# Feed-forward up units: one 512-column product for both operand parts, halves added on VectorE; two norms' squares summed on VectorE

## The reference

```python
def rms_norm(x, g):
    xf = x.astype(jnp.float32)
    y = xf * lax.rsqrt(jnp.mean(xf * xf, axis=-1, keepdims=True) + EPS)
    return (y * g.astype(jnp.float32)).astype(x.dtype)

def swiglu(h, w_in, w_out):          # w_in 1024 x 5632, w_out 2816 x 1024
    a, b = jnp.split(h @ w_in, 2, axis=-1)
    return (jax.nn.silu(a) * b) @ w_out

h = rms_norm(x, norm_mix_g);  x = x + hybrid_mixer(h, ...)
h = rms_norm(x, norm_x_g);    x = x + cross_attention(h, mem, ...)
h = rms_norm(x, norm_ffn_g);  x = x + swiglu(h, ffn_in_w, ffn_out_w)
```

## Time and profile before

| | |
|---|---|
| median of 3 runs | 1534.67 us (1533.29 to 1534.72) |
| the profiled execution | 1533.79 us |
| its span, first to last instruction | 1532.0 us |
| TensorE busy | 1513.5 us (99%), 10782 products |
| weight load busy | 1409.8 us (92%) |
| VectorE busy | 1143.9 us (75%) |
| ScalarE busy | 812.7 us (53%) |
| granted TensorE clock | 1.000 |

### The profile page before, as it was taken

One profiled execution on the slowest core, in us unless ns is written; L12 is line 12 of the kernel. 1 busy time (PEld: TensorE's weight loads), 2 busy tenths in 40 slices (PEclk: granted clock), 3 DMA queues, 4 the chain that ended last, 5 costly groups with the idle time before them and its releaser, 6 DMA issues.

```text
span 1532.0 us, 30888 instructions
## 1 busy us (share of the span) xinstructions
PE 1513.5 (99%) x10782; PEld 1409.8 (92%) x10782; DVE 1143.9 (75%) x2384; ACT 812.7 (53%) x1456; POOL 270.9 (18%) x363
## 2 busy tenths in 40 slices
PE   8999999999999999999999999999999999999998
PEld 7999887999999998899999999999999888888886
DVE  5799998764666666868999976888888666666665
ACT  6545778554544446655565564333334545454454
POOL 2010441000100000000000006888885000000000
PEclk9999999999999999999999999999999999999999
DMA  7674433543565554433555564444445565655563
GB/s 257 191 254 127 142 114 122 192 156 124 180 199 180 184 179 153 149 132 106 175 187 183 168 202 155 144 142 137 137 138 165 192 192 193 194 193 194 194 194 110
DMA packets 71146, 257.78 MB, mean 168 GB/s; under 512 B 8304, under 2 KB 8512, under 8 KB 70816
## 3 DMA queue, kind: packets, MB, share of 16 engines
q1 hardware_dynamic: 68112, 246.97, 50.0%
q0 software_dynamic: 2960, 9.86, 2.0%
HBM read 254.67 MB, written 1.08 MB: 167 GB/s over the span
## 4 chain that ended last, share of the span: by engine, by line
PE 90%; DVE 5%; ACT 3%; issue 1%; DMA 0%; DVEq 0%; ACTq 0%
PE bank L368 18%; PE bank L369 18%; PE bank L370 18%; PE bank L986 8%; PE bank L987 8%; PE bank L988 8%; PE bank L969 4%; DVE arena L1758 1%; PE bank L441 1%; DVE ring_lo L1661 1%; PE bank L442 1%; PE bank L443 1%; PE bank L457 1%; PE bank L380 1%; ACT ring_hi L1135 1%
## 5 line engine op out<-in xcount | busy, mean ns | idle before, releaser
L1661 DVE TENSOR_TENSOR ring_lo<-ring_raw,ring_hi 128x1024 fp32r<-128x1024 f32 x459 | 562.6, 1229 | 178.2 <-ACT ring_hi L1135 175.2
L368 PE MATMUL bank<-operand_hi,ring_hi 128*128 128x256 f32 x2144 | 618.1, 288 | 8.1 <-DVE ring_lo L1720 7.5
L369 PE MATMUL bank<-operand_lo,ring_hi 128*128 128x256 f32 x2144 | 607.1, 283 | 0.0
L370 PE MATMUL bank<-operand_hi,ring_lo 128*128 128x256 f32 x2144 | 607.1, 283 | 0.0
L1135 ACT ACTIVATE ring_hi<-ring_raw 128x1024 fp32r<-128x1024 f32 x459 | 480.1, 1049 | 76.0 <-PE bank L370 64.6
L368 PEld LDWEIGHTS bank<-operand_hi,ring_hi 128*128 128x128 f32 x2144 | 411.6, 192 | 10.6 <-DVE ring_lo L1720 7.5
L369 PEld LDWEIGHTS bank<-operand_lo,ring_hi 128*128 128x128 f32 x2144 | 412.0, 192 | 0.3
L370 PEld LDWEIGHTS bank<-operand_hi,ring_lo 128*128 128x128 f32 x2144 | 411.5, 192 | 0.0
L1119 POOL TENSOR_SCALAR onehots<-iota_k,routeT 128x128 f32<-128x128 f32 x256 | 207.1, 824 | 230.7 <-ACT routeT L1584 193.9
L986 PE MATMUL bank<-ring_hi,hidden_hi 128*128 128x512 f32 x512 | 199.3, 389 | 0.4 <-DVE hidden_lo L2301 0.4
L987 PE MATMUL bank<-ring_lo,hidden_hi 128*128 128x512 f32 x512 | 199.2, 389 | 0.0
(11 more groups left out here) (295 smaller groups left out, 1703.2 us busy)
## 6 DMA issues: line engine op xcount, KB each, us to landing
ring_raw<-in_stream SPq DMA_DIRECT2D x467, 512.0 KB, 3.5
arena<-bias_rows POOLq DMA_DIRECT2D x8, 384.0 KB, 3.9
arena<-in_memT SPq DMA_DIRECT2D x2, 512.0 KB, 4.9
arena<-in_xT POOLq DMA_DIRECT2D x1, 1024.0 KB, 7.4
arena<-in_w POOLq DMA_DIRECT2D x2, 512.0 KB, 9.8
arena<-in_memT POOLq DMA_DIRECT2D x1, 1024.0 KB, 5.4
out_rows<-arena SPq DMA_DIRECT2D x4, 256.0 KB, 2.0
arena<-arena POOLq DMA_DIRECT2D x4, 128.0 KB, 4.6
```

The costliest lines, as they stand in the source:

```text
L368: pe.matmul(out, wh, xh, start=start, stop=False, **kw)
L369: pe.matmul(out, wh, xl, start=False, stop=False, **kw)
L370: return pe.matmul(out, wl, xh, start=False, stop=stop, **kw)
L1661: dve.tensor_tensor(w_lo[:, slot, 0:n], raw[:, slot, 0:n], (raw if n == 1 else w_hi)[:, slot, 0:n].bitcast(F32), ALU.subtract)\
```

## The change

In the feed-forward up units the high and low operand parts become two halves of one tile, so that one product of 512 columns with the high weights fills both halves of a bank; the low weights' product is added to the left half. In the eviction VectorE first adds the two halves of the bank (a reduce over pairs of columns 256 apart), waits for its own write, and then multiplies the sum by `std` out of SBUF. The semaphores that silu and the gated product wait for are new ones, signalled by that second instruction; `bank_free` is signalled by the first.

For N_MIX and N_X VectorE adds the eight chunks of squares in three instructions (1024, 512 and 256 columns) and TensorE makes one product of ones by the sum instead of eight. The other norms keep the eight products (`norm_by_chunk`). In the cross-attention the order on TensorE changes: query unit 2, norm, query unit 3, scores 0 instead of norm, query unit 2, scores 0, query unit 3.

```diff
-        a_hi = sb("operand_hi", [P, KC, S], F32R)
-        a_lo = sb("operand_lo", [P, KC, S], F32R)
+        a_parts = sb("operand_parts", [P, 2, KC, S], F32R)
+        a_hi, a_lo = a_parts[:, 0, :, :], a_parts[:, 1, :, :]
+        SUMMED = (N_MIX, N_X)
...
+            def side_by_side(b, slot, c, start, stop):
+                c0 = slice(c * P, (c + 1) * P)
+                pe.matmul(bank[b][:, :].rearrange("p (a s) -> p a s", a=2), w_hi[:, slot, c0], a_parts[:, :, c, :],
+                          start=start, stop=False, skip_group_check=True)
+                return pe.matmul(bank[b][:, 0:S], w_lo[:, slot, c0], a_hi[:, c, :], start=False, stop=stop, skip_group_check=True)
...
-            def norm(k, b=3):
+            def norm_by_chunk(k, b):
                 take(b, ("norm", k))
                 for c in range(KC):
                     pe.wait_ge(norm_sq, SQUARED[k] + c + 1 if k else 1)
                     m = pe.matmul(bank[b][:, 0:S], ones[:], sq[:, c, :], start=c == 0, stop=c == KC - 1)
                 m.then_inc(norm_sum, 1)
+            def norm(k, b=3):
+                take(b, ("norm", k))
+                pe.wait_ge(squares_added, SUMMED.index(k) + 1)
+                pe.matmul(bank[b][:, 0:S], ones[:], sq[:, 0, :], start=True, stop=True).then_inc(norm_sum, 1)
...
             project_two(U["xq"], (4, 5), O_X)
+            x_query(2)
             norm(N_X)
-            x_query(2)
+            x_query(3)
             x_scores(0)
-            x_query(3)
...
# ffn_up, on TensorE
                 for c in range(KC):
-                    c0 = slice(c * P, (c + 1) * P)
-                    m = three(bank[b][:, 0:S], w_hi[:, slot, c0], w_lo[:, slot, c0], a_hi[:, c, :], a_lo[:, c, :],
-                              c == 0, c == KC - 1)
+                    m = side_by_side(b, slot, c, c == 0, c == KC - 1)
...
-            project_two(u0, (4, 5), O_FFN)
-            norm(N_FFN)
+            project_two(u0, (4, 5), O_FFN, halves=True)
+            norm_by_chunk(N_FFN, 3)
...
# ScalarE
-            def ffn_silu(par, n):
-                act.wait_ge(bank_free[4 + 2 * par], n)
+            def ffn_silu(par, f):
+                act.wait_ge(ffn_scaled, f + 1)
                 act.activation(act2[:, par, :], act2[:, par, :], ACT.Silu).then_inc(silu_done, 1)
...
# VectorE
+            def add_squares(k):
+                dve.wait_ge(norm_sq, SQUARED[k] + KC if k else 1)
+                after(dve.tensor_tensor(sq[:, 0:4, :], sq[:, 0:4, :], sq[:, 4:8, :], ALU.add))
+                after(dve.tensor_tensor(sq[:, 0:2, :], sq[:, 0:2, :], sq[:, 2:4, :], ALU.add))
+                dve.tensor_tensor(sq[:, 0, :], sq[:, 0, :], sq[:, 1, :], ALU.add).then_inc(squares_added, 1)
...
             dve.memset(brow[0:NH, 0:S], FAR).then_inc(brow_sb, 1)
+            add_squares(N_MIX)
             dve.wait_ge(consts_in, 48)
...
                 lo_to(FIRST_USE[k] + RING - 1)
+                if summed is not None:
+                    add_squares(summed)
-            tail_rest("wout", wout_bank, O_X, G_X)
+            tail_rest("wout", wout_bank, O_X, G_X, N_X)
...
+            def halves_of(b):
+                return bank[b][:, :].rearrange("p (a s) -> p s a", a=2)
-            def ffn_pre(u, par):
+            def ffn_pre(u, par, n):
                 dve.wait_ge(unit_done, u + 1)
-                dve.tensor_tensor(act2[:, par, :], bank[4 + 2 * par][:, 0:S], std[:], ALU.mult)\
-                   .then_inc(bank_free[4 + 2 * par], 1)
+                dve.tensor_reduce(act2[:, par, :], halves_of(4 + 2 * par), AX, ALU.add).then_inc(bank_free[4 + 2 * par], 1)
+                dve.wait_ge(bank_free[4 + 2 * par], n)
+                dve.tensor_tensor(act2[:, par, :], act2[:, par, :], std[:], ALU.mult).then_inc(ffn_scaled, 1)
             def ffn_gate(u, par, f, n):
                 dve.wait_ge(unit_done, u + 2)
-                dve.tensor_tensor(gate[:, par, :], bank[5 + 2 * par][:, 0:S], std[:], ALU.mult)\
-                   .then_inc(bank_free[5 + 2 * par], 1)
+                dve.tensor_reduce(gate[:, par, :], halves_of(5 + 2 * par), AX, ALU.add).then_inc(bank_free[5 + 2 * par], 1)
+                dve.wait_ge(bank_free[5 + 2 * par], n)
+                dve.tensor_tensor(gate[:, par, :], gate[:, par, :], std[:], ALU.mult).then_inc(ffn_gated, 1)
                 dve.wait_ge(silu_done, f + 1)
-                dve.wait_ge(bank_free[5 + 2 * par], n)
+                dve.wait_ge(ffn_gated, f + 1)
                 dve.tensor_tensor(act2[:, par, :], gate[:, par, :], act2[:, par, :], ALU.mult).then_inc(ffn_prod, 1)
```

More of the change, by code:

```diff
@@ L212, in build @@
         norm_sq = sem("norm_sq")
+        squares_added = sem("squares_added")
         col_sum = sem("col_sum")
@@ L217, in build @@
         ffn_prod = sem("ffn_prod")
+        ffn_scaled = sem("ffn_scaled")
+        ffn_gated = sem("ffn_gated")
         norm_sum = sem("norm_sum")
@@ L401, in project_cols, with chunk_of, project_two @@
                 m.then_inc(unit_done, 1)
-            def chunk_of(u, b, c):
+            def chunk_of(u, b, c, halves):
                 c0 = slice(c * P, (c + 1) * P)
-                m = three(bank[b][:, 0:S], w_hi[:, u % RING, c0], w_lo[:, u % RING, c0], a_hi[:, c, :], a_lo[:, c, :],
-                          c == 0, c == KC - 1)
+                if halves:
+                    m = side_by_side(b, u % RING, c, c == 0, c == KC - 1)
+                else:
+                    m = three(bank[b][:, 0:S], w_hi[:, u % RING, c0], w_lo[:, u % RING, c0], a_hi[:, c, :], a_lo[:, c, :],
+                              c == 0, c == KC - 1)
                 if c == KC - 1:
                     m.then_inc(unit_done, 1)
-            def project_two(u, banks, first):
+            def project_two(u, banks, first, halves=False):
                 unit(u)
@@ L417, in project_two @@
                         chunk_ready(first, c)
-                        chunk_of(u, banks[0], c)
+                        chunk_of(u, banks[0], c, halves)
                     for c in (2 * half, 2 * half + 1):
-                        chunk_of(u + 1, banks[1], c)
+                        chunk_of(u + 1, banks[1], c, halves)
             def project_rows(u0, b, name, first=None):
@@ L908, in _ @@
                 if n == 1:
-                    norm(N_PEER, 7)
+                    norm_by_chunk(N_PEER, 7)
                 if n == 9:
@@ L1438, in ffn_hi @@
                 act.activation(h_hi[:, par, :], act2[:, par, :], ACT.Copy).then_inc(hid_hi, 1)
-            n0 = base["ffn"]
             hi(u0 + RING - 1, (u0 + RING - 1) % RING)
@@ L1444, in _ @@
             norm(N_FFN)
-            ffn_silu(0, n0[0] + 1)
+            ffn_silu(0, 0)
             hi(u0 + RING, (u0 + RING) % RING)
@@ L1451, in _ @@
                     hi(i * 12 + (u + 3), (u + 3) % RING)
-                    ffn_silu(par, i * 2 + (n0[2 * par] + 1 + (k + 1) // 2))
+                    ffn_silu(par, i * 4 + (k + 1))
                     hi(i * 12 + (u + 4), (u + 4) % RING)
@@ L1459, in _ @@
             hi_to(u + RING)
-            ffn_silu(1, n0[2] + 1 + f // 2)
+            ffn_silu(1, f)
             hi_to(u + 1 + RING)
@@ L1924, in rest_bank, with tail_rest @@
                                              ALU.mult, ALU.subtract).then_inc(opnd_ready, 1)
-            def tail_rest(name, landed_bank, k, gain):
+            def tail_rest(name, landed_bank, k, gain, summed=None):
                 lo_to(FIRST_USE[k] + RING - 2)
@@ L2022, in _ @@
             rstd(("norm", N_FFN))
-            ffn_pre(u0, 0)
+            ffn_pre(u0, 0, n0[0] + 1)
             ffn_gate(u0, 0, 0, n0[1] + 1)
@@ L2030, in _ @@
                     lo(i * 12 + (u + 3), (u + 3) % RING)
-                    ffn_pre(i * 12 + u, par)
+                    ffn_pre(i * 12 + u, par, i * 2 + (n0[2 * par] + 1 + (k + 1) // 2))
                     lo(i * 12 + (u + 4), (u + 4) % RING)
@@ L2039, in _ @@
             lo_to(u + RING)
-            ffn_pre(u, 1)
+            ffn_pre(u, 1, n0[2] + 1 + f // 2)
             ffn_gate(u, 1, f, n0[3] + 1 + f // 2)
```

## The result

The changed kernel takes 1544.24 us (median of 4 runs, 1542.1 to 1544.61) against 1534.58 us before: 1.006 times, 95% interval 1.0047 to 1.0073, so 9.7 us slower. The forecast was 1540.5 us in a range of 1535 to 1556, which is 6.7 us over the execution that it started from. The profiled execution has a span of 1542.8 us, 10.8 us over that of before.

The account below looks back on a forecast made before the run. TensorE was taken as the bound, with a VectorE-ScalarE ring close behind that the change makes the pace-setter: 1533.79 + 10.6 (feed-forward stage) - 1.8 - 2.05 (two norms) = 1540.5 us, range 1535 to 1556.

Parts of the forecast that it names:

- a ring of VectorE and ScalarE: Feed-forward loop: the VectorE-ScalarE chain grows from 7.57 to 9.03 us a step, over TensorE's 8.43, and sets the pace.
- about 0.6 us a step: Feed-forward loop: TensorE stands idle 0.6 us in each step, most likely before the down unit.
- The price of an eviction: Feed-forward evictions: each grows by 0.73 us, a 0.69 us reduce plus a 0.04 us dependent start.
- Rival (b): Evictions: reducing pairs 256 columns apart costs more than an in-order read, up to 1564 us; chance 0.15 for 1549 or more.
- Rival (a): Feed-forward stage: TensorE stays the bound and the change gains, 1525.2 us, if the ring stays under 8.43 us; chance 0.09.
- Rival (c): The two norms: they give nothing because what they free on TensorE is waited away, 1544.4 us; chance 0.08.
- the stage's 10.6 us: Feed-forward stage: the next stage starts at about 594.4 us instead of 583.83, a loss of 10.6 us.
- The first eviction of the loop: Start of the feed-forward loop: moves from 406.04 to about 406.6 us, bounds 405.8 and 407.3.
- The wide product: Up units: one 512-column product replaces two of 256, 0.0135 us less a chunk, 4.7 us if TensorE stayed the bound.
- The norms: First and second norm: one product of ones replaces eight, saving 1.8 us at the first and 2.05 at the second.
- The late root: First norm: ScalarE's table load lets the root start only 1.6 us earlier, so TensorE waits 1.2 us for low operand.
- my list of signs: Expected trace signs, among them TensorE waits of about 1.2 us near 35 us and half a microsecond at the transposes.

Follow-up runs that it names:

- e3_order: The changed kernel with ScalarE's rounding of the next weight unit moved ahead of the silu; 1529.82 us, ratio 0.9966.
- e1_norms: The changed kernel with the feed-forward stage put back, so only the two norms' part remains; 1530.26 us, ratio 0.997.
- e8_fill: The changed kernel with five unused fp32 products on TensorE between the last two down units; 1542.85 us, ratio 1.0055.
- e5_wide: Norms and wide product with the old left-half eviction, so the high-weights, low-operand product is left out of the result; 1527.84 us, ratio 0.9956.
- e13_oldorder: The norms alone, but with the old order of query units and scores at the second norm; 1532.77 us, ratio 0.9986.
- e7_extra2: The kernel before with two more unused VectorE products, each waited for, in each eviction; 1555.28 us, ratio 1.0138.
- e12_best: The change with rounding ahead of silu, earlier root table, hidden low part first in the last step, and one-run operand layout; 1528.67 us, ratio 0.9962.

## Why the prediction was right, and by how much it was off

The direction, the mechanism and the range were right, but the loss was forecast about a third too small: 6.7 us, against 9.7 us between the medians and 10.8 us between the two profiled executions.

**The pace of the stage.** This was right: a ring of VectorE and ScalarE, 7.57 us long, with 1.07 us to spend, sets the pace once it is longer than TensorE's step. Three runs change that length: one more product stays under the threshold and is not to be told from free, two are over it and cost 21 us, and a swap on ScalarE that takes the silu and its wait out of the ring gives the loss back with all of VectorE's work left in place. VectorE's load, which is as high in `e3_order` (1177.3 us busy) as in the change, is not the cause. TensorE loses about 0.6 us a step (9.10 - 8.54), as forecast, and in the place that was named.

**The price of an eviction.** The reduce took 0.684 us, against 0.69 forecast. Rival (b), a dearer read of columns 256 apart, fell: the rows of a bank read in order have 0.692. With it falls what I had weighed from the Trainium skill ("Advanced Engine Details and Errata", PSUM cachelines), as far as VectorE goes; the page speaks of matmuls. Rival (a) had its condition right: with the eviction of before the wide product gains, by 2.4 us. Rival (c), that the norms give nothing, had forecast 1544.4 us, within 0.2 us of what was measured; that is chance, for `e1_norms` shows that the norms give 4.6 us.

**The term that was off: the stage's 10.6 us.** From the norm ahead of the stage to the first product behind it the stage took 13.9 us more (392.23 to 594.36 after, 395.62 to 583.83 before). Three pieces make the difference. A step is 9.10 us and not 9.03: the gated product starts 0.10 us behind the gate's product, where the kernel before has 0.03 in the loop. Two waits stand ahead of it in both kernels, so their number doesn't explain it, and the cause stays open; 20 x 0.07 = 1.5 us. The first eviction of the loop came 0.3 us later than I let it. And the last down unit starts 4.35 us behind the last reduce, where I had 4.2, and takes 4.44 us, where I had 2.9: I had summed the chain to it but not a fall of TensorE's clock behind it, 1.5 us of slower starts (16 x 0.093 us) in this execution, which are absent in `e8_fill`. The forecast named 594.4 us for the next stage and the trace has 594.36; that is luck, since the forecast counted from a stage that starts where it did before, and it starts 3.4 us earlier.

**The wide product.** Forecast 0.0135 us a chunk, measured 0.0065; 2.4 us in `e5_wide` in place of 4.7. That did no harm to the forecast, as TensorE wasn't the bound.

**The norms.** For the first, -1.8 us was forecast; the norm starts 0.6 us later in this execution and `uconv` 1.17 us earlier, which is -1.8. The 0.6 us are from the start, where the clock rose later (TensorE's starts are 0.21 us apart until 13.2 us, and until 11.7 us before); nothing in the change touches that, and in `e1_norms`, whose start is the same, it rose at 11.3 us. For the second, -2.05 was forecast and -3.25 + 1.02 = -2.23 measured (transposes, against the 1.02 us that the stage's start was ahead). The late root and the wait ahead of `uconv` (1.07 us, forecast 1.2) are there as forecast. The half microsecond forecast at the transposes is 0.22 us there; 0.49 us are waited at the scores, which my list of signs didn't name.

**Together**, in the profiled pair: +0.6 at the start, -1.8 and -2.2 at the norms, +13.9 in the stage, +0.3 elsewhere, 10.8 us. Forecast were -3.85 and +10.6, from 1533.79 to 1540.5.

## What to carry to other kernels

Before adding work to an engine with idle time, ask what that idle time waits for: when it waits for a partner that waits for it, the reserve is the bound's step minus the length of the ring, and beyond that point each added instruction counts in full, in every step. A ring can be shortened without taking any work out, by moving onto the partner's queue, ahead of the dependent instruction, what is ready anyway. And at the end of a stage, a chain that leaves TensorE idle for two microseconds can cost the slower level of its clock on top, as it did in two of three such places in these traces.

## What the runs showed of the hardware that I had not expected

- A reduce with 256 results out of 512 bank columns, pairs 256 columns apart, takes 0.684 us: no more than a reduce of the same 512 columns to 2 results (0.692).
- A 512-column product followed by a 256-column one takes 0.353 us for both, 0.007 more than 0.227 + 0.12, and whether the wide one reads one run or two makes no difference (1527.66 and 1527.84 us).
- After 2.21 and 2.25 us of idle time TensorE went to 1.2 GHz for 3.4 us (within 0.2 us of its return in the change, 1.2 us behind it in `e13_oldorder`); after 2.59 us in `e7_extra2` it stayed at 2.4 GHz, and so it did with 2.3 us of products in the gap.
- In the traces of `e3_order`, `e12_best` and `e13_oldorder` the clock was also at 1.2 GHz for 6.8 us, from 655.6, 656.1 and 658.8 us, a few microseconds behind the first 64-column products of the next block; the ten other traces have the full clock there. These three executions took 2.1, 3.8 and 2.4 us more than the median of their kernel.
- The gated product, which reads what the VectorE instruction before it wrote, starts 0.03 us behind that one's end in the loop of the kernel before and 0.10 us in that of the change, with two waits ahead of it in both.
